# Ten pairs of unused 512-column products in a two-layer transformer block on one core

## The reference, cut to what matters

```python
# first block
z = rms_norm(x) @ w_in                                 # 2048 -> 13,000-odd columns, four branches and gates
h = x + mixed @ w_out                                  # residual "out"
v = rms_norm(h)
h = h + (silu(v @ w_gate) * (v @ w_up)) @ w_down       # gated unit, DFF = 5632; residual "down"
# second block
proj = rms_norm(h) @ w_in_2                            # two attention branches and gates
h = h + mix @ w_out_2                                  # residual "out2"
h = h + cross_attention(h, mem) @ w_xo                 # residual "xo"
# experts: routing queries, keys, top-16 of 16,384 experts for each of 8 heads
q = rms_norm(h) @ w_pq
h = h + sum_over_chosen(gelu(xn . u[e]) * g) * v[e]    # computed densely: all u rows, then all v rows
return rms_norm(h)
```

## Time and profile before

| | |
|---|---|
| median of 3 runs | 4129.48 us |
| lowest and highest | 4114.68 and 4171.09 us |
| profiled execution, first to last instruction | 4184.8 us |
| the profiled execution's own time | not given apart from its span |
| TensorE products | 33,866 records, busy 97% of the span |
| VectorE, ScalarE | busy 56% and 49% |
| mean granted clock of TensorE | 0.984 |

### The profile page before, as it was taken

The page is one execution under the profiler, slowest core; times in us unless marked ns, Lnnn a source line. Parts: engine busy times, 40 slices in busy tenths (PEclk is TensorE's granted clock), DMA queues, the critical chain, the costliest instruction groups (busy, mean ns, idle before and its releaser), DMA issues.

```text
span 4184.8 us, 82601 instructions
## 1 busy us (share of the span) xinstructions
PE 4055.4 (97%) x33866; PEld 4006.7 (96%) x33866; DVE 2362.8 (56%) x3414; ACT 2064.4 (49%) x3097; POOL 33.4 (1%) x61
## 2 busy tenths in 40 slices
PE   7999999999999998999999999999999999999998
PEld 6999999999999998999999999999999999999998
DVE  5655565454444456544665666897854454444444
ACT  5554554455555444445554444447754444444443
POOL 0000000000000000000000000000000000000000
PEclk9999999999999999999999999999999999999999
DMA  4545555545555554443434444555555555655553
GB/s 171 175 168 172 172 181 182 180 152 188 183 187 184 181 193 154 169 164 122 146 137 165 167 151 138 177 190 173 181 191 189 182 190 202 209 201 175 186 186 125
DMA packets 111183, 726.00 MB, mean 173 GB/s; under 512 B 11296, under 2 KB 11424, under 8 KB 29184
## 3 DMA queue, kind: packets, MB, share of 16 engines
q1 hardware_dynamic: 105904, 701.55, 48.7%
q0 software_dynamic: 5072, 21.50, 1.6%
HBM read 712.52 MB, written 10.49 MB: 173 GB/s over the span
## 4 chain that ended last, share of the span: by engine, by line
PE 95%; DVE 2%; ACT 2%; issue 1%; DMA 0%; DVEq 0%; SPq 0%; ACTq 0%
PE ps L489 19%; PE ps L494 19%; PE ps L490 19%; PE ps L542 9%; PE ps L544 9%; PE ps L549 9%; PE ps L572 1%; PE ps L969 1%; PE ps L607 1%; PE ps L515 1%; PE ps L516 1%; PE ps L517 1%; PE ps L625 1%; DVE tmp L1647 1%; ACT wh L1029 1%
## 5 line engine op out<-in xcount | busy, mean ns | idle before, releaser
L1588 DVE TENSOR_TENSOR wl<-raw,wh 128x1024 fp32r<-128x1024 f32 x1328 | 1616.8, 1225 | 1584.3 <-ACT wh L1029 1579.7
L1029 ACT ACTIVATE wh<-raw 128x1024 fp32r<-128x1024 f32 x1328 | 1401.1, 1059 | 1847.2 <-PE ps L542 656.4
L489 PE MATMUL ps<-x,wh 128*128 128x256 f32 x6784 | 1648.6, 283 | 41.6 <-DVE x L1641 25.1
L490 PE MATMUL ps<-x,wh 128*128 128x256 f32 x6784 | 1633.2, 281 | 0.0
L489 PEld LDWEIGHTS ps<-x,wh 128*128 128x128 f32 x6784 | 1290.8, 190 | 51.2 <-issue 44.8
L490 PEld LDWEIGHTS ps<-x,wh 128*128 128x128 f32 x6784 | 1289.1, 190 | 0.6
L494 PE MATMUL ps<-x,wl 128*128 128x256 f32 x6784 | 934.5, 281 | 2.5 <-DVE wl L1588 2.5
L494 PEld LDWEIGHTS ps<-x,wl 128*128 128x128 f32 x6784 | 857.9, 190 | 2.8 <-DVE wl L1588 2.8
L542 PE MATMUL ps<-xkh,wh 128*128 128x256 f32 x3328 | 802.1, 281 | 29.1 <-DVE xkl L1599 27.2
L544 PE MATMUL ps<-xkl,wh 128*128 128x256 f32 x3328 | 801.5, 281 | 0.0
L542 PEld LDWEIGHTS ps<-xkh,wh 128*128 128x128 f32 x3328 | 634.2, 191 | 30.1 <-issue 30.1
(11 more groups left out here) (338 smaller groups left out, 2188.0 us busy)
## 6 DMA issues: line engine op xcount, KB each, us to landing
raw<-in_w_in SPq DMA_DIRECT2D x184, 1024.0 KB, 4.9
raw<-in_expert_u SPq DMA_DIRECT2D x128, 1024.0 KB, 4.9
raw<-in_expert_v SPq DMA_DIRECT2D x128, 1024.0 KB, 4.9
raw<-in_w_ffn_gate SPq DMA_DIRECT2D x44, 1024.0 KB, 4.8
raw<-in_w_ffn_up SPq DMA_DIRECT2D x44, 1024.0 KB, 4.8
raw<-in_w_ffn_down SPq DMA_DIRECT2D x44, 1024.0 KB, 4.9
raw<-in_w_out SPq DMA_DIRECT2D x32, 1024.0 KB, 4.8
raw<-in_w_branch SPq DMA_DIRECT2D x16, 1024.0 KB, 5.1
```

The source lines that it names most:

```text
L489: begin(mm(o, wh[:, j, c], x_h[:, kc, :], start=kc == 0, stop=False), kc % 8 == 0)
L490: mm(o, wh[:, j, c], x_l[:, kc, :], start=False, stop=False)
L1029: f(wh[:, u % 4, 0:width], raw[:, ring, c:c + width], ACT.Copy).then_inc(*k.up("hi"))
L1588: v.tensor_tensor(wl[:, u % 4, 0:width], raw[:, ring, c:c + width], wh[:, u % 4, 0:width].bitcast(F32), ALU.subtract).then_inc(*k.up("lo"))
```

## The change

A helper `wide` issues two products of 128 weight columns and 512 moving columns, both read from the current slot of `wh`, into one whole bank. Each has start and stop set, so it overwrites the bank. The bank is 7. In a residual the pair is issued in the first input tile, ahead of the product that itself overwrites bank 7 (t == 14). In a tile it is issued in the second half chunk between the `wh` and the `wl` products, after `reserve(7)`, and nothing reads it. There are ten pairs: one in each of the six residuals, one in the first tile of the gated unit, of the routing queries and of u1, and one in the second tile of u0. The first turn of the loops "ffn" and "u1" is written out ahead of the loop, so that the pair runs once.

```diff
+            def wide(j, b):
+                for _ in range(2):
+                    mm(ps[:, b, :], wh[:, j, 0:P], wh[:, j, 16:16 + 2 * T], start=True, stop=True)
...
-            def tile_T(b, reader="a", x_h=xh, x_l=xl):
+            def tile_T(b, reader="a", x_h=xh, x_l=xl, spare=None):
...
+                    if spare is not None and kc0:
+                        reserve(spare)
+                        wide(j, spare)
                     low()
...
+                        if first and t == 14:
+                            wide(j, 7)
                         begin(mm(o, wh[:, j, c], xkh[:, x, :], start=first and t % 2 == 0, stop=False,
...
-            with k.loop("ffn", pe, FT // 2):
+            for f in range(2):
+                reserve(4 + f)
+                tile_T(f, spare=None if f else 7)
+                tile_T(4 + f, "v")
+            with k.loop("ffn", pe, FT // 2 - 1):
...
             for h in range(8):
-                tile_T(0)
+                tile_T(0, spare=None if h else 7)
...
             for c in range(HALF):
-                tile_T(c % 2)
+                tile_T(c % 2, spare=7 if c == 1 else None)
...
-            with k.loop("u1", pe, 8):
+            for b in range(8):
+                tile_T(b % 2, spare=None if b else 7)
+            with k.loop("u1", pe, 7):
                 for b in range(8):
                     tile_T(b % 2)
```

## The result

The changed kernel takes 4200.97 us (4186.39 to 4206.24, 4 runs) against 4129.47 (4114.68 to 4171.09, 4 runs). The ratio is 1.0146, interval 1.0090 to 1.0203: slower by 1.5%. The forecast was 4104 us.

The account below looks back on a forecast made before the run. TensorE, busy 97% of the span, was taken to bound the kernel. 4184.8 - 69.9 (slow products turned fast) + 4.3 (pairs) = 4119 us of span, shifted to 4092 to 4112, taken as 4104; range 4088 to 4160 at 0.8.

Parts of the forecast that it names:

- the long stretches of the kernel before can fall either way from run to run: Stretches behind low-clock gaps (out, ffn, down, out2, xo, v0 with u1, v1) fall fast or slow, 76.3 us in all.
- The price per product: In TensorE's unbroken stretches, a slow product costs 4.45 ns more than a fast one, 3.8%.
- No wait at the pair in u1: In u1, bank 7's last read ends 2.6 us before the pair; wait counted zero, at most 1 us.
- the whole effect is under 2%: Whole kernel: net gain 69.9 - 4.3 = 65.6 us, 1.6% even against the slowest execution shown.
- the cadence change only at something other than a 256-column float32r product: Within a TensorE stretch the cadence is latched, changing only where another kind of product interrupts; 113.3 or 117.8 ns.
- the group L642: Float32 group in the projections, 215 ns products, said to exchange the cadence every time; cited for a rival sharing 33%.
- I take the fast end: All ten pairs leave their streams fast: 15,708 products gain 4.45 ns each, 69.9 us; 50%, 4104 us.
- Rival 2: Every pair leaves the stretch behind it slow in every run: 4185 us, 1.4% slower, range 4175 to 4195; 9%.
- from the profiled execution to the metric: Whole kernel: timed runs lie 7 to 27 us under the profile's scale, middle 17; span 4119 becomes 4092 to 4112.
- the sum for all places fast: Whole profiled execution with every pair leaving fast: 4184.8 - 69.9 + 4.3 = 4119 us of span.
- The price of a pair: At each of ten places, two 512-column products at 215 ns each on TensorE's path; 4.3 us in all.
- a single gap for each width: Rival on all ten pairs: no second cadence, only 20 x 215 ns cost, 4134 us; 33% together with another rival.

Follow-up runs that it names:

- ladder c: Kernel before plus unread groups in u0 tiles 2 to 29: 512-column pair amid wh, then amid wl products, one, then two extra 256-column products; no time given.
- ladder a: Kernel before plus one, two, three, then four unread 512-column products between wh and wl products, seven u0 tiles each (tiles 2 to 29); no time given.

## Why the prediction was wrong

**Right.** Two cadences at full clock, 113.3 and 117.8 ns, latched over long stretches, in every kernel run here. That the long stretches of the kernel before can fall either way from run to run, shown by running it again: the same code fell the other way in five of them. The price per product: the spans less 4.45 ns per slow product (and 4.7 or 2.8 or 1.9 us of pairs) come to 4115.6 and 4113.3 for the two profiles of the kernel before, 4184.7 - 68.8 - 4.7 = 4111.2 for the changed one, 4196.1 - 76.3 - 2.8 = 4117.0 with residual pairs only, 4170.0 - 52.0 - 1.9 = 4116.1 with tile pairs only. Spans 63 us apart fall within 6. No wait at the pair in u1: right. That the whole effect is under 2%: right.

**Read too widely.** The prediction has the cadence change only at something other than a 256-column float32r product. One such product more, reading `wh`, exchanged it in seven of seven tiles of ladder c. And the group L642 does not exchange every time: the one at 45.9 us of the changed kernel stands between products 117 to 119 ns apart on both sides.

**The step that failed** is "I take the fast end": that a stream given slack in its weight loads settles into the fast cadence. The products of the change, which start 16 elements into the slot, left a fast stream slow in 20 of 20 cases, and a slow one fast only from one of its kinds, 14 cases of 31. The kernel paid for that with 68.8 us of slow stretches where the prediction had put none behind a pair. Slack is not what decides: pairs with the same slack and a start at 32 left fast from either class, and one extra product of 256 columns, with no slack at all, changed the class too. Rival 2 named this outcome, with 9%, at 4175 to 4195; it held in its main clause, with eight of ten places slow in the profile, though the routing queries and u1 came out fast. Its time was too low by the shift that follows.

**The second step that failed** is the shift "from the profiled execution to the metric". I read the distance of 7 us and more between the all-fast sum and the lowest timed run as another scale of the profile. There is none: in every profiled run for which both are on record the device time is the span plus 1.7 to 2.2 us, 1.7 in that of the changed kernel. The first profile was an unlucky draw, and the twelve runs of the kernel with the start at 32 still differ by 9 us. Without the shift of 17 us the sum for all places fast was 4119 us, and the kernel that does put all places fast has 4117.76. Rival 2 would have been 4202 against a measured 4200.97, but part of that closeness is luck: its sum has u1 slow, 13.7 us, and the one profiled execution, with u1 fast, took 4186.39.

**A term mis-sized, without weight.** The price of a pair was 0.47 us (233 and 236 ns to the next start), not 0.43: 215 ns was the nearest row, a record of 256 columns in plain float32.

**The reason it went against the change** and not with it is the draw: the kernel before is fast by chance in some of its long stretches, the changed one is slow in nearly all of them, by the rule of the start. The profile of the kernel before that the prediction used had 69 us of slow stretches against it already (its span of 4184.8 equals that of the changed kernel, 4184.7), and the two profiles side by side would have shown nothing. The Trainium skill, "TensorE: Matmul & The Clock Gate", section "Back-to-back issue gap", gives 215.8 ns for 512 columns from start to start, for a product by itself; the pairs here took 233 and 236 out of a fast stream, and by a single gap for each width the change would have cost 4.3 us and not 1.5%.

**Open.** What in TensorE holds the cadence; why the start of the moving columns modulo 256 bytes sets it; how the kinds of slow stream differ, apart from the first interval of a wide product in them. Whether the start of the weights matters too, and whether the period is 256 bytes at other places than the pair compared above, was not tried. Whether a shift of the activations themselves would keep the whole kernel fast was not tried.

## What to carry to other kernels

Divide time by count in stretches where TensorE is never idle: a busy share of 97% hid 3.8% per product. If a kernel's runs spread by over 1%, take a second profile of the same kernel before explaining anything by one: what differs between them is chance, and a change has to be judged against the draw and not against one execution. A group of products that is there only to set a state has to be measured from each state it may meet; here one number, the start of its moving operand, made the difference between 1.5% slower and 0.4% faster.

## What the runs showed of the hardware that was not expected

At a granted clock of 2.4 GHz a stream of 128-column loads and 256-column float32r products holds one of two cadences, 113.3 or 117.8 ns, over thousands of products and across hardware loops. An extra product or pair between them can set it. What a pair of 512-column products sets depends on where its moving columns start modulo 256 bytes, and not on the form of the access, the place, or which of the 128-column blocks tried the weights were: at 0 it keeps (14 of 14), at 32, 128 and 192 bytes it leaves fast (one exception in 49 cases at 192, none in 28 at 128 and 7 at 32), at 64 it leaves a fast stream slow in every case. The number counts as well: a single such product from 64 bytes left slow in seven of seven tiles of ladder a, while one of 256 columns from there exchanged in seven of seven. Two transposes of the identity left a fast stream slow in five of five places of a kernel and three of three of a ladder, though the transposes of the kernel before (its L502) left a fast stream fast in 11 of the 16 cases that the starts of the first profile show.
